# A hybrid decoder block on one core: order of the loads in the mixing stage, a ring of four instead of eight input buffers in the feed-forward stage, and a later place for the adds that finish the first half

## The reference

```python
mix = jnp.concatenate([o_attn, o_conv], axis=-1) @ w_o
x = x + g1 * mix
h2 = rms_norm(x, norm2_g) * (1 + sc2) + sh2
x = x + g2 * (jnp.square(jax.nn.relu(h2 @ w_ff1)) @ w_ff2)
```

## Time and profile before

| | |
|---|---|
| median of 3 runs | 2916.45 us (2915.93 to 2917.53) |
| profiled execution | 2916.45 us, span 2914.7 us |
| TensorE busy with matmuls | 2763.4 us, 95% of the span |
| VectorE, ScalarE, GpSimd busy | 1298.7, 963.3 and 638.1 us |
| mean granted TensorE clock | 0.971 of 2.4 GHz |
| mixing stage | about 1160 to 1435 us |
| feed-forward stage | about 1438 to 2915 us, second run from 2158 |

### The profile page before, as it was taken

One profiled execution on the slowest core, in us unless ns is written; L12 is line 12 of the kernel. 1 busy time (PEld: TensorE's weight loads), 2 busy tenths in 40 slices (PEclk: granted clock), 3 DMA queues, 4 the chain that ended last, 5 costly groups with the idle time before them and its releaser, 6 DMA issues.

```text
span 2914.7 us, 40311 instructions
## 1 busy us (share of the span) xinstructions
PE 2763.4 (95%) x15122; PEld 2301.6 (79%) x15122; DVE 1298.7 (45%) x3268; ACT 963.3 (33%) x2349; POOL 638.1 (22%) x415
## 2 busy tenths in 40 slices
PE   4999989979999977999799999999999999999998
PEld 1788858857777753688588888888889999999998
DVE  3248889857777633788521122211143222222223
ACT  2434413545665532456412211122231222112220
POOL 0000000000000000566233333333322333333331
PEclk6899989989999998999899999999999999999999
DMA  6667626646644368467413131131433311111113
GB/s 245 195 220 243 206 99 228 216 145 203 185 165 150 117 222 329 133 200 229 128 59 101 51 102 51 44 108 44 135 125 104 105 48 44 50 45 44 51 44 112
DMA packets 284198, 387.95 MB, mean 133 GB/s; under 512 B 25738, under 2 KB 233978, under 8 KB 277854
## 3 DMA queue, kind: packets, MB, share of 16 engines
q1 hardware_dynamic: 261458, 294.87, 31.2%
q0 software_dynamic: 5072, 81.05, 7.8%
q10 hardware_dynamic: 17476, 9.47, 1.1%
HBM read 308.72 MB, written 148.74 MB: 157 GB/s over the span
## 4 chain that ended last, share of the span: by engine, by line
PE 50%; DVE 0%; ACT 0%; issue 0%; DVEq 0%
PE ff_u_ps L2404 17%; PE ff_u_ps L2405 17%; PE ff_u_ps L2406 17%; PE ff_out_ps L2400 0%; DVE gluT L2334 0%; DVE ff_x_t L2334 0%; DVE ff_h_lo L2322 0%; DVE ff_sqr L2334 0%; PE ff_u_ps L2400 0%; ACT ff_w_hi L2277 0%; DVEq L2180 0%; DVE ff_y L2345 0%; ACT ff_h_hi L2286 0%; DVE ff_y L2351 0%
## 5 line engine op out<-in xcount | busy, mean ns | idle before, releaser
L2404 PE MATMUL ff_u_ps<-ff_h_hi,ff_w_hi 128*128 128x352 f32 (+1 forms) x1280 | 450.6, 352 | 10.7 <-DVE ff_h_lo L2322 10.7
L2405 PE MATMUL ff_u_ps<-ff_h_lo,ff_w_hi 128*128 128x352 f32 (+1 forms) x1280 | 449.2, 351 | 0.0
L2406 PE MATMUL ff_u_ps<-ff_h_hi,ff_w_lo 128*128 128x352 f32 (+1 forms) x1280 | 448.8, 351 | 0.0
L2404 PE MATMUL ff_u_ps<-ff_a_hi,ff_w_hi 128*128 128x352 f32 (+1 forms) x1280 | 448.7, 351 | 0.0
L2405 PE MATMUL ff_u_ps<-ff_a_lo,ff_w_hi 128*128 128x352 f32 (+1 forms) x1280 | 448.2, 350 | 0.0
L2406 PE MATMUL ff_u_ps<-ff_a_hi,ff_w_lo 128*128 128x352 f32 (+1 forms) x1280 | 447.8, 350 | 0.0
L2252 POOL TENSOR_TENSOR ff_w_lo<-gluT,ff_w_hi 128x1024 fp32r<-128x1024 f32 x128 | 307.3, 2401 | 557.7 <-ACT ff_w_hi L2277 557.7
L2362 DVE TENSOR_TENSOR ff_sqr<-gluT 128x352 f32<-128x352 f32 (+1 forms) x160 | 98.8, 618 | 621.4 <-ACT gluT L2305 621.4
L2345 DVE SCALAR_TENSOR_TENSOR ff_y<-ff_u_ps,modT,ff_y 128x512 f32<-128x512 f32 (+2 forms) x280 | 178.7, 644 | 432.4 <-PE ff_u_ps L2406 432.4
L2277 ACT ACTIVATE ff_w_hi<-gluT 128x1024 fp32r<-128x1024 f32 x128 | 134.9, 1054 | 622.4 <-PE ff_u_ps L2406 610.1
L2404 PEld LDWEIGHTS ff_u_ps<-ff_h_hi,ff_w_hi 128*128 128x128 f32 x1280 | 240.8, 188 | 34.7 <-POOL ff_w_lo L2252 11.2
(11 more groups left out here) (270 smaller groups left out, 4310.4 us busy)
## 6 DMA issues: line engine op xcount, KB each, us to landing
gluT<-in_w_ff_dram SPq DMA_DIRECT2D x128, 512.0 KB, 3.8
out_new_k_sample_dram<-in_cache_k_dram POOLq DMA_DIRECT2D x8, 4088.0 KB, 15.5
out_new_v_sample_dram<-in_cache_v_dram POOLq DMA_DIRECT2D x8, 4088.0 KB, 15.5
dwq<-in_w_ada_dram SPq DMA_DIRECT2D x32, 512.0 KB, 7.4
gluT<-in_cache_k_dram SPq DMA_DIRECT2D x16, 1024.0 KB, 12.0
sa_vn<-in_cache_v_dram SPq DMA_DIRECT2D x16, 1024.0 KB, 15.0
mx_acc<-acc_d SPq DMA_DIRECT2D x16, 768.0 KB, 8.5
vu_x_in<-in_x_prompt_dram SPq DMA_DIRECT2D x16, 512.0 KB, 6.1
```

The lines of the kernel that those rows point to most:

```text
L2404: pe.matmul(out, w_hi[:, b, w], hi, start=first, stop=False)
L2405: pe.matmul(out, w_hi[:, b, w], lo, start=False, stop=False)
L2406: return pe.matmul(out, w_lo[:, b, w], hi, start=False, stop=last)
```

## The change

In SP's list of the mixing stage, `load_acc` and `load_x` become one function `load_rest`, called with the same i: turn i is now conv(i), acc(i), x(i), and the last call for tile 16 goes. The ring of h2 pieces has four places instead of eight, with four semaphores; in turn 10 only four pieces are loaded ahead, and the feed-forward stage loads the other twelve of its first run. `ff_act` moves within `hold`, and the buffer `sqr`, which had its own 4 KB per partition, now lies in `hold` too. In the second run's first block, VectorE does `finish` of tile j after the squares of group j+2 instead of j+1; TensorE's list is as before.

```diff
--- before.py
+++ after.py
@@ -151,7 +151,7 @@
         acc_in = [whole.enter_context(nc.semaphore(f"acc_in{i}")) for i in range(2)]
         dw_in = [whole.enter_context(nc.semaphore(f"dw_in{i}")) for i in range(2)]
         ff_w_ld = [whole.enter_context(nc.semaphore(f"ff_w_ld{i}")) for i in range(2)]
-        ff_h_in = [whole.enter_context(nc.semaphore(f"ff_h_in{i}")) for i in range(8)]
+        ff_h_in = [whole.enter_context(nc.semaphore(f"ff_h_in{i}")) for i in range(4)]
         wp_in, wl_in = whole.enter_context(nc.semaphore("wp_in")), whole.enter_context(nc.semaphore("wl_in"))
 
         def copy_cache(eng, n):
@@ -228,9 +228,9 @@
             wl_raw = hold[:, CC * CW:CC * (CW + D)].rearrange("p (k c) -> p k c", k=CC)
             wpT = hold[:, CC * (CW + D):CC * (2 * CW + D)].rearrange("p (k c) -> p k c", k=CC)
             ff_raw = hold[:, 0:2 * D].rearrange("p (a c) -> p a c", a=2)
-            HR = 8
-            ff_h = hold[:, 2 * D:2 * D + HR * ((SEQ // 2 + NS) // 2)].rearrange("p (a c) -> p a c", a=HR)
-            ff_act = hold[:, 7 * D - 512:8 * D - 512].rearrange("p (a c) -> p a c", a=2)
+            ff_h = hold[:, 2 * D:2 * D + 4 * ((SEQ // 2 + NS) // 2)].rearrange("p (a c) -> p a c", a=4)
+            ff_act = hold[:, 4 * D + 512:5 * D + 512].rearrange("p (a c) -> p a c", a=2)
+            ff_sqr = hold[:, 5 * D + 512:6 * D + 512].rearrange("p (a c) -> p a c", a=2)
 
             def ff_load_up(sp, f, slot):
 
@@ -1700,7 +1700,7 @@
                             sp.wait_ge(S["dw_pe"], i - 1)
                         sp.dma_start(dwt[:, i % 2, :, 0:n], dw_d[:, :, i * P:i * P + n]).then_inc(dw_in[i % 2], 16)
 
-                    def load_acc(i):
+                    def load_rest(i):
                         n = rows_of(i)
                         t = slice(i * P, i * P + n)
                         if i >= 2:
@@ -1710,39 +1710,32 @@
                         elif i == NT:
                             sp.wait_ge(os_out, 16 * DB)
                             sp.dma_start(acc[0:n, i % 2, 0], os_d).then_inc(acc_in[i % 2], 16)
-
-                    def load_x(i):
-                        n = rows_of(i)
-                        t = slice(i * P, i * P + n)
                         if i >= 2:
                             sp.wait_ge(S["x1_d_"], i - 1)
                         src = I["x_prompt"][0, t, :] if i < NT else I["x_sample"].rearrange("b t d -> (b t) d")
                         sp.dma_start(x_in[0:n, i % 2], src).then_inc(x_in_s[i % 2], 16)
 
-                    load_x(0)
+                    load_rest(0)
                     for n in range(WU):
                         if n >= 2:
                             sp.wait_ge(S["w_lod"], n - 1)
                         sp.dma_start(w_raw[:, n % 2], I["w_o"][0, n * P:(n + 1) * P, :]).then_inc(w_ld[n % 2], 16)
                         if n == 1:
-                            load_x(1)
+                            load_rest(1)
                             sp.dma_start(gate_p[:], mod_d[8:9, 2 * D:3 * D].to_broadcast([P, D])).then_inc(S["gate_in"], 16)
                             sp.dma_start(gate_s[:], bass.AP(mod_d.tensor, 2 * D, [[NMOD, DB], [0, DS], [1, D]])).then_inc(S["gate_in"], 16)
                             sp.dma_start(gate_b[:], I["b_ada"][:, 2 * D:3 * D].to_broadcast([P, D])).then_inc(S["gate_in"], 16)
                     for i in range(2, NT + 1):
                         load_conv(i)
-                        load_acc(i)
-                        if i >= 3:
-                            load_x(i - 1)
+                        load_rest(i)
                         if i == 10:
                             sp.wait_ge(S["wf_pe"], NF)
                             for f in range(2):
                                 ff_load_up(sp, f, f)
                             for par in range(2):
                                 sp.wait_ge(h2_out[par], 16 * 2)
-                            for k in range(KT):
+                            for k in range(4):
                                 sp.dma_start(ff_h[:, k, 0:512], h2_d[:, k, 0:512]).then_inc(ff_h_in[k], 16)
-                    load_x(NT)
                     sp.wait_ge(S["h2_d_"], NT + 1)
                     sp.dma_start(h2_d[:, :, SEQ:TOK], h2[:, NT % 2, :, 0:NS]).then_inc(h2_out[NT % 2], 16)
                     for s in (x1_out, h2_out):
@@ -2087,8 +2080,7 @@
             FB = 4
             NBLK = FF // P // FB
             MAXT = SEQ // 2 + NS
-            w_raw, h_raw, relu = ff_raw, ff_h, ff_act
-            sqr = sb("sqr", [P, 2, 512])
+            w_raw, h_raw, relu, sqr = ff_raw, ff_h, ff_act, ff_sqr
             w_hi = sb("w_hi", [P, 2, D], F32R)
             w_lo = sb("w_lo", [P, 2, D], F32R)
             y = sb("y", [P, KT, MAXT])
@@ -2100,6 +2092,7 @@
             out_ps = ps("out_ps", [P, D])
             XR = 4
             x1_t = sb("x1_t", [P, XR, D])
+            HR = 4
 
             def sm(name):
                 return sem("ff_" + name)
@@ -2169,7 +2162,7 @@
                     return x1_t[0:flat[j][1], j % XR]
                 spare = h_raw.rearrange("p a t -> p (a t)")
                 return (spare[:, 0:D], spare[:, D:2 * D], relu.rearrange("p a t -> p (a t)"),
-                        sqr[:].rearrange("p a t -> p (a t)"), w_raw[:, 0])[j - TAIL][0:flat[j][1]]
+                        sqr.rearrange("p a t -> p (a t)"), w_raw[:, 0])[j - TAIL][0:flat[j][1]]
 
             def out_half(j, half):
 
@@ -2360,8 +2353,8 @@
                                 if e >= 2:
                                     v.wait_ge(alo_d, e - 1)
                                 v.tensor_tensor(sqr[:, e % 2, 0:width], relu[:, e % 2, 0:width], relu[:, e % 2, 0:width], ALU.mult).then_inc(sqr_d, 1)
-                                if run == 1 and blk == 0 and 1 <= e - up_count(1) < 1 + N0:
-                                    finish(e - up_count(1) - 1)
+                                if run == 1 and blk == 0 and 2 <= e - up_count(1) < 2 + N0:
+                                    finish(e - up_count(1) - 2)
                             for e in range(KT * nch):
                                 k, c = divmod(e, nch)
                                 g = groups_before(run * PER_RUN + blk * WT + FB) + e
```

## The result

The changed kernel takes 2988.28 us (median of 4 runs, 2984.69 to 2991.98), the kernel before 2916.8 us in the same series. The ratio is 1.0244, with a 95% interval of 1.0232 to 1.0256: 71.5 us slower, where 74.7 were forecast. The profiled execution has a span of 2985.3 us against 2914.7, 70.6 more.

A forecast was written before the change was run, and what follows sets the result against it. TensorE, busy 95% of the span, was taken as the bound. Mixing stage 51.2, feed-forward start 6 and later adds 17.5 sum to 74.7 us on 2916.45: 2991.2 us, range given 2958 to 3012 us.

The forecast's parts named there:

- The mixing stage's loop: Mixing stage: acc is requested only after a residual, so its landing enters a 16.99 us period; stage +51.2 us.
- The give-back after residual 13: End of mixing stage: only the small sample tile is left to merge, TensorE is ahead, 1.5 us come back.
- Turn 10's interval: Mixing stage, turn 10: weight and h2 loads issued before acc(11) make one interval longer, +5.5 us once.
- TensorE's idle time per period: Mixing stage, a sign of the forecast: TensorE idles about 3 us per tile.
- The landing and the h2 store: Mixing stage: h2's store falls after acc's landing, so 8.0 us is taken instead of 8.4; otherwise 5.2 us dearer.
- The ring: Feed-forward start: four h2 buffers instead of eight delay the second weight tile, +6 us, chosen between 3.9 and 8.4.
- nothing is late at the turn to the second run: Feed-forward, turn to second run: SP's weight loads wait longer but still arrive in time, cost 0.
- The adds: Second run's first block: TensorE's transposes wait seven times 2.5 us for VectorE's later adds, +17.5 us.
- Rival (b): TensorE's clock falls in the seven new waits, 2.5 us each, 17.5 us more, 3009 us; chance 0.12.
- (a): Mixing stage: acc lands faster, in 5.9 us; period 14.9, stage +24, total 2964 us; chance 0.12.
- (c): Mixing stage: TensorE stays the bound, GpSimd's idle time swallows the landing; 2940 us; chance 0.05.
- (d): Feed-forward stage: not slower, as moved buffers let 7680 matmuls run closer, each gaining 9.7 ns; chance 0.03.

The follow-up runs named there:

- the changed kernel with acc mended: The changed kernel with acc(i+1) issued ahead of the wait of x(i), conv(i+1) and x(i) staying late: 2944.28 us, ratio 1.0086 against the kernel before.

## Why the prediction was right

**The mixing stage's loop** was the right mechanism. The wait that was named came, at the place named, and it goes away when the acc load alone is issued earlier. Its size was 43.4 us against 51.2 forecast. Three terms were off. The landing was taken as 8.0 us and comes to 7.75 in the average period; the merge, counted with its hand-overs, took 5.43 instead of 5.52 plus 0.09; so the period was 16.54 instead of 16.99, 5.4 us over twelve turns. The give-back after residual 13 was taken as 1.5 us and was 3.9: one shortened interval was counted, and two came, by 2.2 and 1.7 us. Turn 10's interval was 22.46 us, where 16.99 + 5.5 = 22.49 were counted. TensorE's idle time per period, forecast at about 3 us, is 13.5 / 6.65 = 2.0 us in the records. A record of a 128x512 matmul lasts 0.40 us there while the next starts 0.24 us after it, so the last record before a wait covers part of it.

**The landing and the h2 store.** The medians from 1230 to 1340, in the kernel before and twice in the changed one:

```profile
mx_acc<-acc_d SPq DMA_DIRECT2D x8, 768.0 KB, 8.4
...
mx_acc<-acc_d SPq DMA_DIRECT2D x7, 768.0 KB, 7.6
...
h_d<-mx_h ACTq DMA_DIRECT2D x6, 512.0 KB, 3.5
```

The h2 store took 9.4 us before. It is now issued after acc has landed, and both got faster. This is what was taken from the earlier trace rows, and more of it than assumed; no run moves the store alone.

**The ring** was forecast at 6 and was 6.7 in the changed kernel's profile, 5 by the time of the ring alone. The 6 was a choice between 3.9 and 8.4, and its reason did not come true: SP issues x1's loads only at 1500.33, behind all twelve pieces. So the size is in part luck. That nothing is late at the turn to the second run was right.

**The adds** were forecast at 17.5 us and were 19.2: seven periods longer by 2.5 us, and one fall of the clock, which made one group 1.5 us longer. Rival (b), a fall at each of the seven for 2.5 us each, thus came true at one, for 1.5 us; in the kernel with this part alone it was two, in the changed kernel with acc mended one. It is not shown what decides which wait is followed by a fall; all seven are alike in length.

**The other rivals.** (a) needed 5.9 us of landing, which came only when acc stood first in the queue. (c) is refuted by the waits. (d), closer matmuls, did not occur: with the parts taken out the time returns to that of the kernel before.

**The sum.** The forecast is 3 to 4 us off in the whole, but 7.8 us in its largest term. The ring (0.7), the adds (1.7) and the later start of the stage (1.5, not a part of the change) went the other way and hid half of that, which is luck. The forecast's own range was also stated wider than its terms give: with 44.7 or 59 us for the stage and 3.9 or 8.4 for the ring it is 2982.6 to 3001.4 us, not 2978 to 3004. The measured time lies in both.

## What to carry to other kernels

A load's place in an in-order queue is set by the waits ahead of it, not by its own: moving one load by one turn moved another, which was wanted at once, behind a wait. Ask of each moved wait what stands behind it, and close the loop: if a buffer is asked for only when its user is ready, the full landing enters the period. When two engines share a single buffer, a step in one list has to move with its partner in the other; moved together they cost nothing, the adds alone cost 20 us.

## What was not expected of the hardware

The landing of a 768 KB load was not shortened by putting 256 KB behind it instead of ahead, when both were issued within half a microsecond (7.7 against 7.6 us), but it was by putting 512 KB more behind it (5.9 us).

GpSimd and VectorE slow each other in SBUF by more than was counted: 1.6 instead of 1.28 us for a GpSimd add of 128 x 512, and 2.79 instead of some 0.7 us for a VectorE product, which twice ended 0.55 us after the GpSimd instruction that it had met. A fall of TensorE's clock followed some waits of 2.31 us and not others of the same length: one of seven in two traces, two of seven in a third.
